# A hybrid decoder step on one core: the per-head values are turned into token rows by VectorE in 32x32 blocks instead of by TensorE

## The reference, cut to what matters

```python
q = silu(qa); sig = sigmoid(fa)
k = (1 - lb) * (1 - sig); logf = log(lb + (1 - lb) * sig)
v = ia                                    # the projection itself, per head 1056 tokens x 128
b = cumsum(logf)                          # within a chunk
att = einsum('thk,shk,tshk->hts', q, k, exp(b[t] - b[s]) where t >= s)
o = att @ v + (q * exp(b)) @ S
S_new = exp(b_last) * S + (k * exp(b_last - b)).T @ v
```

## Time and profile before

| | |
|---|---|
| three runs | 1320.48, 1321.42, 1322.83 us |
| the profiled execution | 1320.63 us, span 1318.8 us |
| mean granted TensorE clock | 0.984 |
| VectorE busy | 594.2 us, 45%, 1237 instructions |
| ScalarE busy | 517.5 us, 39%, 1019 instructions |
| GpSimd busy | 260.9 us, 20%, 119 instructions |
| the costliest group | projection matmuls of line 968, 67% of the chain that ended last |

### The profile page before, as it was taken

The page is one execution under the profiler, slowest core; times in us unless marked ns, Lnnn a source line. Parts: engine busy times, 40 slices in busy tenths (PEclk is TensorE's granted clock), DMA queues, the critical chain, the costliest instruction groups (busy, mean ns, idle before and its releaser), DMA issues.

```text
span 1318.8 us, 23470 instructions
## 1 busy us (share of the span) xinstructions
PE 1287.5 (98%) x9148; PEld 1227.6 (93%) x9148; DVE 594.2 (45%) x1237; ACT 517.5 (39%) x1019; POOL 260.9 (20%) x119
## 2 busy tenths in 40 slices
PE   5999999999999999999999999999999899999998
PEld 4999999999999999999999999999999899999885
DVE  6645657574847465600000155555556202345132
ACT  7463535445353535511111255555554324114111
POOL 0222221222322222222222111111110121342000
PEclk9999999999999999999999999999999899999999
DMA  6212121202021221121112311111100312241330
GB/s 198 67 33 66 36 65 34 80 18 80 18 80 37 76 58 41 35 64 48 48 35 49 85 33 32 32 32 32 32 16 1 106 32 64 62 98 33 119 125 37
DMA packets 136750, 73.61 MB, mean 56 GB/s; under 512 B 37185, under 2 KB 133138, under 8 KB 136690
## 3 DMA queue, kind: packets, MB, share of 16 engines
q1 hardware_dynamic: 136706, 72.99, 20.0%
HBM read 63.77 MB, written 10.22 MB: 56 GB/s over the span
## 4 chain that ended last, share of the span: by engine, by line
PE 93%; DVE 3%; ACT 2%; DMA 1%; issue 1%; SPq 0%; POOL 0%; DVEq 0%; ACTq 0%
PE pj L968 67%; PE pj L984 3%; PE pj L1328 3%; DVE scores L1617 2%; PE ps_a L1328 1%; PE ps_e L1328 1%; PE ps_d L1098 1%; PE ps_a L1169 1%; PE ps_d L1208 1%; PE ps_e L1208 1%; PE ps_b L1196 1%; PE ps_d L1328 1%; PE ps_b L1328 1%; PE ps_c L1328 1%; PE ps_c L1080 1%; PE ps_c L1196 1%
## 5 line engine op out<-in xcount | busy, mean ns | idle before, releaser
L968 PE MATMUL pj<-xn_h,w_h 128*128 128x352 f32 x1704 | 565.5, 332 | 3.4 <-DVE xn_l L1384 1.9
L968 PE MATMUL pj<-xn_h,w_l 128*128 128x352 f32 x1704 | 554.3, 325 | 0.0
L968 PE MATMUL pj<-xn_l,w_h 128*128 128x352 f32 x1704 | 553.5, 325 | 0.0
L558 POOL TENSOR_TENSOR w_l<-w_raw,w_h 128x1024 fp32r<-128x1024 f32 x82 | 203.3, 2479 | 688.8 <-ACT w_h L630 688.8
L968 PEld LDWEIGHTS pj<-xn_h,w_h 128*128 128x128 f32 x1704 | 325.8, 191 | 12.7 <-ACT w_h L630 3.5
L968 PEld LDWEIGHTS pj<-xn_l,w_h 128*128 128x128 f32 x1704 | 326.4, 192 | 0.3
L968 PEld LDWEIGHTS pj<-xn_h,w_l 128*128 128x128 f32 x1704 | 325.6, 191 | 0.0
L630 ACT ACTIVATE w_h<-w_raw 128x1024 fp32r<-128x1024 f32 x82 | 86.4, 1054 | 114.7 <-PE pj L968 100.1
L1565 DVE TENSOR_TENSOR mg<-sg,pj 128x352 f32 (+1 forms) x24 | 12.4, 522 | 151.9 <-PE pj L968 150.4
L835 ACT ACTIVATE scores<-scores,stat 128x256 f32<-128x256 f32 (+1 forms) x128 | 61.4, 481 | 0.0
L968 PE MATMUL pj<-hl_l,w_h 128*128 128x352 f32 x168 | 54.2, 323 | 0.0
(11 more groups left out here) (362 smaller groups left out, 2005.4 us busy)
## 6 DMA issues: line engine op xcount, KB each, us to landing
w_raw<-in_w_in_dram SPq DMA_DIRECT2D x132, 256.0 KB, 3.4
x_t<-in_x_prompt_dram SPq DMA_DIRECT2D x8, 512.0 KB, 8.5
s<-in_state_hgrn_dram SPq DMA_DIRECT2D x8, 512.0 KB, 4.2
out_dram<-s SPq DMA_DIRECT2D x8, 512.0 KB, 3.2
w_raw<-in_w_pa_dram SPq DMA_DIRECT2D x16, 256.0 KB, 3.0
w_raw<-in_w_pb_dram SPq DMA_DIRECT2D x16, 256.0 KB, 4.5
wo_raw<-in_w_out_dram SPq DMA_DIRECT2D x8, 512.0 KB, 3.8
x_o<-in_x_prompt_dram SPq DMA_DIRECT2D x8, 512.0 KB, 4.1
```

The lines of the kernel that those rows point to most:

```text
L558: g.tensor_tensor(w_l[p][:], w_raw[p][:], w_h[p][:].bitcast(F32), ALU.subtract).then_inc(w_lo_ready, 1)
L968: mm = nc.tensor.matmul(pj[g][:, 0:W], w[:, kt, :], x[:, kt, span(g)], start=(kt == 0 and m == 0), stop=(kt == KT - 1 and m == 2))
```

## The change: what it does

The nine TensorE turns of the values in each head are gone, and so are the three ScalarE copies of the slots to `vT` and the three ScalarE copies of the turned banks to `v_tok`. In their place VectorE reads each slot of `B(0)` in its PSUM bank with its transpose instruction, which turns 32x32 blocks: for a slot g it runs over four groups of 32 channels (`iv`) and, inside that, over the four groups of 32 partitions that the tokens go to (`jt`); each instruction reads 32 partitions and two or three 32-token blocks (64 or 96 elements a partition; twelve with 96 and four with 64 in each slot), and writes 32 partitions of `v_tok`. That is 16 instructions a slot, 48 a head. `turn_values(0)` stands after `ha`, `turn_values(1)` after `kD`, `turn_values(2)` after `m32k`. TensorE's slots of `B(1)` now wait for the last transpose of the slot before them; the products with `v_tok` wait for `v2_33`; ScalarE's `v3_hi` waits for it too. GpSimd waits for its own `split_lo(B(1))` before `v3_lo`.

```diff
-    exponentials = ["v0", "ebl", "ebs", "xkD", "v1", "x64", "x32", "v2", "xdq", "xdk", "xqI"]
-    turned = ["vt0", "vt1", "vts", "v3_hi", "v3_hi2"]
+    exponentials = ["ebl", "ebs", "xkD", "x64", "x32", "xdq", "xdk", "xqI"]
+    turned = ["v3_hi", "v3_hi2"]
...
-    products = ["kD", "m64q", "m64k", "m32q", "m32k", "dqm", "dkm", "qIm", "kt0", "kt1", "kts", "k3_hi", "k3_hi2", "k3_lo"]
+    turned_values = lambda g: [f"v{g}_{i}{j}" for i in range(4) for j in range(4)]
+    products = turned_values(0) + ["kD"] + turned_values(1) + ["m64q", "m64k", "m32q", "m32k"] + turned_values(2) + ["dqm", "dkm", "qIm", "kt0", "kt1", "kts", "k3_hi", "k3_hi2", "k3_lo"]
...
                 g.wait_ge(act_done, act.at(now, "v3_hi2"))
+                g.wait_ge(w_lo_ready, B(1)[0] + 1)
...
-                v_copy(0)
...
-                v_copy(1)
...
-                v_copy(2)
...
-                for n, (bank, cols) in enumerate(((ps_a, slice(0, 4)), (ps_b, slice(4, 8)))):
-                    a.wait_ge(pe_done, pe.at(now, f"vt{n}"))
-                    a.activation(v_tok[:, cols, :], bank[:].rearrange("p (c v) -> p c v", c=4), ACT.Copy).then_inc(act_done, act.tick(now, f"vt{n}"))
-                a.wait_ge(pe_done, pe.at(now, "vts"))
-                a.activation(v_tok[0:NS, NC, :], ps_e[0:NS, 0:P], ACT.Copy).then_inc(act_done, act.tick(now, "vts"))
-                a.wait_ge(act_done, act.at(now, "vts"))
+                a.wait_ge(dve_done, dve.at(now, "v2_33"))
...
-                gate_slot(1, "v", (act_done, act), 0)
-                t.wait_ge(act_done, act.at(now, "v2"))
-                turn(ps_a, 0, vT, range(0, 4), "vt0")
-                turn(ps_b, 0, vT, range(4, 8), "vt1")
-                turn(ps_e, 0, vT, [NC], "vts")
-
+                gate_slot(1, "v", (dve_done, dve), 0)
                 t.wait_ge(dve_done, dve.at(now, "kD"))
                 turn(ps_c, 0, kD, range(0, 4), "kt0")
                 turn(ps_d, 0, kD, range(4, 8), "kt1")
-                t.wait_ge(act_done, act.at(now, "vts"))
                 turn(ps_e, P, kD, [NC], "kts")
-                gate_slot(1, "v", (act_done, act), 1)
+                gate_slot(1, "v", (dve_done, dve), 1)
...
-                gate_slot(1, "v", (act_done, act), 2)
-
-                t.wait_ge(act_done, act.at(now, "vts"))
+                gate_slot(1, "v", (dve_done, dve), 2)
+
+                t.wait_ge(dve_done, dve.at(now, "v2_33"))
...
+                def turn_values(g):
+
+                    v.wait_ge(slot_done, head_blocks(i)(0)[0] * 3 + (g + 1))
+                    blocks = pj[g][:, 0:W].rearrange("p (b t) -> p b t", t=32)
+                    n = W // 32
+                    for iv in range(4):
+                        for jt in range(4):
+                            first = (jt - n * g) % 4
+                            c = (n * g + first) // 4
+                            many = len(range(first, n, 4))
+                            v.transpose(v_tok[32 * jt:32 * jt + 32, c:c + many, 32 * iv:32 * iv + 32],
+                                        blocks[32 * iv:32 * iv + 32, first:n:4, :]).then_inc(dve_done, done(f"v{g}_{iv}{jt}"))
...
+                turn_values(0)
                 v.wait_ge(dve_done, dve.at(prev, "q2"))
 
                 need(act, act_done, "xkD")
                 tt(kD[:], kD[:], k[:], ALU.mult).then_inc(dve_done, done("kD"))
+                turn_values(1)
...
+                turn_values(2)
                 need(act, act_done, "xdk")
```

More of the change, by code:

```diff
@@ L158, in hybrid_step @@
     ])
-    head_products = ["vt0", "vt1", "vts", "kt0", "kt1", "kts", "p0", "p1", "ps", "u0", "u1",
+    head_products = ["kt0", "kt1", "kts", "p0", "p1", "ps", "u0", "u1",
                      "o0", "o1", "os", "us0", "us1", "ms0", "ms1", "mss"]
@@ L701, in head @@
                 split_hi(B(1))
-                def v_copy(g):
-                    a.wait_ge(slot_done, B(0)[0] * 3 + (g + 1))
-                    a.activation(vT[:, span(g)], pj[g][:, 0:W], ACT.Copy).then_inc(act_done, act.tick(now, f"v{g}"))
                 def exp(name, need, out, src, scale=1.0):
@@ L1035, in gate_slot @@
                         return
-                    step = f"k{g}" if last and k_block == 2 else f"{name}{g}"
+                    step = f"k{g}" if last and k_block == 2 else f"v{g}_33" if name == "v" else f"{name}{g}"
                     t.wait_ge(by[0], by[1].at(now, step))
```

## The result

Four runs of the changed kernel gave 1374.94 to 1377.33 us, a median of 1376.06; four of the kernel before gave a median of 1321.99. The ratio is 1.0411, with a 95% interval of 1.0393 to 1.0429: slower by 54 us. The forecast was 1368, with a range of 1345 to 1404.

A forecast was written before the change was run, and what follows sets the result against it. TensorE, busy 98% of the span, was taken to bound the kernel. To 1320.6 us came 33.9 for products starting late behind dkm and 13.2 for clock falls, 1367.7; with 0.8 for the median, 1368 after rounding; range 1345 to 1404.

The forecast's parts named there:

- TensorE bounds, and a wait in a head is lost: In the eight heads, one us less TensorE work is one us of time; one us of TensorE waiting is lost.
- What it removes: 7.9 us: Nine TensorE value turns, 0.99 us a head, 7.9 us in eight heads; the ScalarE copies removed count as nothing.
- The transposes: 13.4 us a head, bounds 7.8 and 17.9: 48 on VectorE a head: 13.4 us with gaps, 7.8 if they overlap, 17.9 if the data part passes twice.
- the copy formula: VectorE transpose cost taken from PSUM copies at 1.05 ns an element: 0.258 us for 96 elements, 0.225 for 64.
- the gap of 0.03: Between VectorE transposes: each writes other partitions than the last, so starts 0.03 us after its end instead of overlapping.
- Where it lies: TensorE stands 5.5 us for dkm; products within a chunk start 4.5 us late in heads 1 to 7, 2.4 in head 0.
- GpSimd beside dqm and dkm: 0.4 us, bounds 0 and 1.90: v3_lo and v_exp start amid VectorE's dqm and dkm and hold them up: 0.4 us, between 0 and 1.90.
- The clock: one more fall, 1.65 us a head: TensorE's stand and the small products bring one added clock fall a head, 13.2 us in all; bounds 0 and 3.8 a head.
- the second stretch that the forecast named as its sign: A second stretch with the clock at 0.5 to 0.7 in each head, behind TensorE's wait for dkm.
- The third rival: TensorE stands, but the clock's fall lands in the stand or replaces the one after the output products: 1355, chance 0.15.
- The sum: Whole kernel: 1320.6 + 33.9 + 13.2 = 1367.7; the runs' median is 0.8 higher, so 1368.5, rounded down to 1368.
- The first two rivals: VectorE transposes overlap, 7.8 us a head: 1313.5, chance 0.14; each is dearer than a copy, 17.9 us: 1404, chance 0.19.

The follow-up runs named there:

- the added part: Kernel before with the 48 transposes a head added, TensorE's value turns kept, GpSimd's v3_lo waiting for v2_33: 1375.56 us; without that wait 1405.93 us.
- the three groups of 16: The change with all transposes at 64 elements: slot 0 stays on one partition group, slot 1 changes only the output's, slot 2 only the input's; 1337.86 us.
- the run with the stand filled: The change plus 24 needless matmuls a head on TensorE between slot 1 of B(1) and the wait for dkm: 1367.63 us.
- the version that beats both: Against the kernel before: VectorE turns value tiles 0 to 4 from vT in 16 transposes, TensorE 5 to 8, GpSimd's v3_lo waits for qIm: 1311.39 us.

## Why the prediction was right, point by point

**TensorE bounds, and a wait in a head is lost.** Right. The waits that the change adds in the heads sum to 46.8 + 3.6 + 2.8 us; the span of the profiled executions grew by 56.7.

**What it removes: 7.9 us.** Right as a price and, as the forecast had it, swallowed by the stand: alone it is gained in full (1.05 us a head for 0.99), and with the added part the time is the same with it and without it (1376.06 and 1375.56).

**The transposes: 13.4 us a head, bounds 7.8 and 17.9.** 14.4. A transpose took 0.271 us on the mean where the copy formula gives 0.258 and 0.225, so turning costs about 0.02 us more than copying; the gap of 0.03 held. That each waits for the last one's end, read from two gaps of 0.04 and 0.02 us, was the step on which the sign hung. Two gaps were thin evidence for it, and the chance of 0.14 for the other side says so; the three groups of 16 bear it out.

**Where it lies.** Right: the wait is for `dkm`, 6.0 us where 5.5 were forecast. The products begin 5.5 us late where 4.5 were forecast (counted from VectorE's last z product: 20.7 us to them before, 26.2 after), and 1.0 of that is the transposes. `v1` was not just in time but 0.4 us late, which the stand for `dkm` absorbs. In head 0 the products begin 5.7 us late where 2.4 were forecast; 1.8 of that is there before the first transpose, and of the rest 1.0 is again the transposes.

**GpSimd beside dqm and dkm: 0.4 us, bounds 0 and 1.90.** 0.26: `dkm` took 1.51 instead of 1.25. The bound was too low. The runs show 4.0 us, where a VectorE product stands through `v_exp` and the weight split together. In the change the product caught so is `qIm`, 5.26 us. Nothing waits for it in time there; in the run with the stand filled it delays `kts`, and TensorE waits 0.4 to 0.5 us for that in the four heads whose products ran at full clock.

**The clock: one more fall, 1.65 us a head.** This is the term that was mis-sized. A fall does come with the stand (products 3.75 us instead of 2.2), but it does not come on top of the old one: the one behind the output products is gone in all eight heads, so the second stretch that the forecast named as its sign is not there. What stands in its place is one stretch, twice as long, whose first 2 us lie in the stand and cost nothing. +1.5, +0.5 and -1.5 leave 0.5 us a head where 1.65 were forecast. The third rival had seen this possibility, with a chance of 0.15, and priced it at nothing; in kind it is what happened, and it was not far from the price either. Also where a fall does come or go by itself, a head changes by 0.8 us and not by 1.65. Two things not in the forecast fill the gap: the transposes' 1.0 us, and 0.5 us for the weight split of `B(3)`, which the slow slot used to cover and the fast one does not. That the errors lie on opposite sides is luck, and it brings the total nearer than the clock's part deserves.

**The sum.** Forecast 47 us, measured 54. Between the two profiled spans it is 56.7: 48.5 from the products of head 0 to those of head 7 (seven times 6.9, where 6.15 were forecast), 5.7 up to the first of these and 2.5 behind the last, where head 7 shows one more low stretch of the clock, near 604 us. The first two rivals are out: the transposes do not overlap, and they are not dearer than a copy by more than 0.02 us.

## What to carry to other kernels

Count instructions, not elements, when VectorE is to move 32x32 blocks across groups of 32 partitions: each start waits for the last end, 0.27 us from start to start for 64 elements and 0.30 for 96, against 0.14 for 64 where the partitions stay. Before work is moved from the engine that bounds to one that has idle time, find the latest moment at which that other engine's results are wanted: 3.9 us of slack a head paid for about a quarter of the 14.4 us that were moved, while the version that moved 5.9 us, in fewer and larger instructions, gained 0.74%, by whole heads 5 us through the turns and 3 through falls of the clock that did not come. When a change may move a fall of the clock, count the falls that it takes away too, and price one by whole heads with it and without it: the slow slot showed 1.65 us, the head 0.8. And look at what a GpSimd instruction will meet after the move: where it starts decided between 1311 and 1348 us.

## What was not expected of the hardware

A VectorE product of two SBUF tensors that GpSimd has once got ahead of can stand through two GpSimd instructions in a row and not only the one in flight: 4.70 us for 0.68, 5.24 and 5.26 for 1.25, ending 0.55, 1.11 and 1.11 us after GpSimd's second instruction, a little less than an unhindered product takes. The reverse is milder: in the change `v_exp`, started behind `dkm`, took 2.79 us instead of 1.90.

How often the clock falls in the heads depends on more than the work that stands at the place: the output products are the same in all kernels, and behind them or elsewhere the heads show eight falls before, five with the turns removed, four in the version that beats both. In the kernel with the stand filled the same 2.1 us wait is followed by products at full clock in three heads and at about half in four. What decides it between one head and the next was not tried.
